# Order of the products of a near down block: pairs of output tiles, high halves first

## The chip, the cores and the metric

The kernel runs on one core of one Trainium2 chip. The metric is the device time of one execution in microseconds; three runs of the kernel before gave 1520.74, 1520.86 and 1521.19 us, the median being 1520.86 us. One more execution was recorded by the hardware profiler; all rows below are from that one.

## The reference, cut to what matters

The reference is a stack of layers over 256 tokens and 1024 features, all in float32. Six of its sublayers are feed-forwards of the same form, with 2816 inner features:

```python
def swiglu(h, w13, w2):
    gate, up = jnp.split(h @ w13, 2, axis=-1)
    return (jax.nn.silu(gate) * up) @ w2
```

Between them stand mixers: four kinds of token mixing in parallel, a gated linear recurrence, and an attention. The change touches the last product of the feed-forwards alone, `hidden @ w2`.

## The kernel before

Activations are held transposed: 128 features on the partitions, 256 tokens along the row. The float32 products are made from halves. A weight block `w` is split into a high half `w_hi` (the value rounded, made by ScalarE, line 666) and a low half `w_lo` (what is left, made by GpSimd, line 571, or by VectorE, line 1105). An activation tile is split in the same way, and both its halves lie side by side, 2 x 256 = 512 columns. A product of one 128x128 weight tile with one activation tile is then two matmuls (`three_products`, lines 1866 and 1867): the high half of the weight against both halves of the activation, 512 columns, and the low half of the weight against the high half of the activation, 256 columns. Both add into the same bank of PSUM, the second into its first 256 columns; VectorE adds the two halves of the bank when it takes the sum out. Below, H is a matmul of the first kind and L one of the second, each with its own weight load.

Weights stream through a ring of six slots (`RING`), one block of up to 128x1024 in each, loaded by SyncE's queue in the order in which TensorE uses them. A slot's semaphore `lo_ready` tells that both halves are made, `used` that TensorE is through with it.

A feed-forward (`ffn` of the TensorE program) goes over 22 chunks of 128 inner features. For a chunk c, `gate_up(c)` makes two tiles from the normed input `xn`: 16 pairs H L, eight for the gate and eight for the up projection, each tile in one bank of PSUM (banks 4 to 7, by turns). ScalarE and VectorE turn these into the hidden tile `hid[:, c]`, split into halves. `down(c)` then calls `near_products`, which multiplies the hidden tile by four of the eight output tiles: the near block, four weight tiles wide, adds into banks 0 to 3, one bank for each output tile d. The other four output tiles are made at the end of the feed-forward from far blocks (`far_products`), from the hidden tiles that are still in memory. The order of the steady part is written out in the code: for k from 0 to 18, `down(k)`, then `gate_up(k + 3)`. After that come `down(19)`, `down(20)`, the first far block, `down(21)`, and the other eleven far blocks. In all there are 6 x 22 = 132 near blocks, with four H and four L in each.

In `near_products` TensorE waits once for the block's low half (and, in `down`, once for the hidden tile), then issues the eight matmuls, and the last of them increments `used`. The order before is H0 L0 H1 L1 H2 L2 H3 L3, the number being the output tile.

Of the kernel before, what the change touches and what calls it, by code (L numbers as in the profile page):

```python
# [11 lines left out]
P = 128  # L12
SEQ = 256
# [5 lines left out]
NFC = FF // P  # L19
# [27 lines left out]
NEAR = HALF // P  # L47
# [21 lines left out]
def near_block(c):  # L69

    return NEAR_LAST if c == NFC - 1 else stored_down(c)
# [141 lines left out]
def slot(n):  # L213

    return n % RING
# [20 lines left out]
def nth_split(n):  # L236

    return SPLITS_SO_FAR[n]
# [34 lines left out]
def build(nc, x_in, blocks, consts, out):  # L273
    ctx = ExitStack()
    with ctx:
        def sb(name, shape, dt=F32):
            return ctx.enter_context(nc.sbuf_tensor(name, shape, dt))
# [6 lines left out]
        w_hi = sb("w_hi", [P, RING, BLK], F32R)  # L284
        w_lo = sb("w_lo", [P, RING, BLK], F32R)
# [19 lines left out]
        hid = nc.alloc_sbuf_tensor_at("hid", [P, NFC, 2, SEQ], F32R, offset=arena_at)  # L305
        ps = ctx.enter_context(nc.psum_tensor("ps", [P, 8, 512], F32))
# [1551 lines left out]
        def _(pe):  # L1858
# [5 lines left out]
            def three_products(where, hi, lo, both, opens, closes):  # L1864

                nc.tensor.matmul(where, hi, both.rearrange("p a t -> p (a t)"), start=opens, stop=False)  # L1866
                return nc.tensor.matmul(where[:, 0:SEQ], lo, both[:, 0, :], start=False, stop=closes)  # L1867
# [65 lines left out]
            def near_products(n0, c):  # L1933

                n = n0 + near_block(c)
                pe.wait_ge(lo_ready[slot(n)], nth_split(n))
                for d in range(NEAR):
                    wh, wl = (w[:, slot(n), d * P:d * P + P] for w in (w_hi, w_lo))
                    ins = three_products(ps[:, d, :], wh, wl, hid[:, c, :, :], c == 0, c == NFC - 1)
                ins.then_inc(used[slot(n)], 1)  # L1940

            def far_products(n0, i):
# [58 lines left out]
            def ffn(f, phase, total=total_squares):  # L2001
# [11 lines left out]
                def down(c):  # L2013
                    pe.wait_ge(h_ready, NFC * f + c + 1)
                    near_products(n0, c)
# [671 lines left out]
```

## Time and profile before

| | us |
|---|---|
| median of 3 runs | 1520.86 (1520.74 to 1521.19) |
| the profiled execution | 1521.21 |
| its span, first to last instruction | 1519.4 |
| TensorE matmuls busy | 1510.9 (99%) |
| TensorE weight loads busy | 1315.8 (87%) |
| VectorE busy | 1052.7 (69%) |
| GpSimd busy | 923.4 (61%) |
| ScalarE busy | 776.9 (51%) |
| TensorE clock granted | 1.000 of full speed over the span |

A matmul's recorded time runs from its start to its modelled end, and matmuls overlap in the pipeline, so the busy share of TensorE says only that there is nearly always one under way. What one matmul costs the engine is the distance from its start to the start of the next one; it is read from a timeline, in which starts are given to 0.01 us.

### The profile page before, as it was taken

The page shows a single profiled execution, that of the slowest core. Times are in us where ns is not written, and L with a number is a line of the kernel's source. Part 1 is how long each engine was busy: PE and PEld are TensorE (multiplying, and loading weights), DVE is VectorE, ACT ScalarE, POOL GpSimd, SP SyncE. Part 2 cuts the span into 40 slices and gives each one's busy share as a digit, 9 for nine tenths or more (in the row PEclk, how much of TensorE's full clock was granted, in tenths as well). Part 3 has the DMA queues.
Part 4 walks back from the last instruction along what each step waited for, and adds up shares of the span by engine and source line. Part 5 has one row for each costly group of instructions (what it writes and reads, how often), then busy time and mean ns, then how long its engine had stood idle before and what let it go on. Part 6 is the DMA issues. An engine that isn't in the chain of part 4 may idle for free.

```text
span 1519.4 us, 24540 instructions
## 1 busy us (share of the span) xinstructions
PE 1510.9 (99%) x9480; PEld 1315.8 (87%) x9480; DVE 1052.7 (69%) x1472; ACT 776.9 (51%) x1125; POOL 923.4 (61%) x1092
## 2 busy tenths in 40 slices
PE   9999999999999999999999999999999999999998
PEld 7888888888888888888899888888888887888887
DVE  7966555666986668976587986655466666797664
ACT  6554441123655455455567655456555456665542
POOL 4966520201687677876766687578776673168663
PEclk9999999999999999999999999999999999999999
DMA  8665633222565564665634565565555562346553
GB/s 302 209 196 183 205 99 115 85 79 86 199 212 183 168 215 160 192 205 165 228 126 167 186 210 185 183 215 187 162 189 189 186 207 94 138 156 207 188 165 119
DMA packets 113491, 263.64 MB, mean 174 GB/s; under 512 B 9184, under 2 KB 51296, under 8 KB 113248
## 3 DMA queue, kind: packets, MB, share of 16 engines
q1 hardware_dynamic: 113376, 262.09, 52.5%
q8 instruction: 75, 1.23, 0.3%
q14 instruction: 40, 0.33, 0.1%
HBM read 261.00 MB, written 1.05 MB: 172 GB/s over the span
## 4 chain that ended last, share of the span: by engine, by line
PE 74%; DVE 1%; ACT 0%; issue 0%; DVEq 0%; ACTq 0%
PE ps L1866 40%; PE ps L1867 21%; PE ps L1961 2%; PE ps L1982 2%; PE ps L1898 1%; PE ps L1899 1%; PE ps L1897 1%; PE ps L2434 1%; PE ps L2436 1%; PE ps L2435 1%; PE ps L2387 1%; PE ps L1997 0%; PE ps L1998 0%; PE ps L1996 0%; DVE arena L1812 0%; PE ps L1929 0%
## 5 line engine op out<-in xcount | busy, mean ns | idle before, releaser
L571 POOL TENSOR_TENSOR w_lo<-raw,w_hi 128x256 fp32r<-128x256 f32 x1056 | 902.4, 887 | 475.1 <-ACT w_hi L666 471.6
L1866 PE MATMUL ps<-xn,w_hi 128*128 128x512 f32 x2112 | 741.2, 393 | 0.4 <-POOL w_lo L571 0.2
L1867 PE MATMUL ps<-xn,w_lo 128*128 128x256 f32 x2112 | 591.4, 280 | 0.0
L666 ACT ACTIVATE w_hi<-raw 128x1024 fp32r<-128x1024 f32 (+1 forms) x516 | 475.5, 932 | 186.0 <-PE ps L1867 146.1
L1866 PEld LDWEIGHTS ps<-xn,w_hi 128*128 128x128 f32 x2112 | 395.1, 187 | 90.1 <-issue 0.7
L1867 PEld LDWEIGHTS ps<-xn,w_lo 128*128 128x128 f32 x2112 | 398.9, 189 | 0.2
L1866 PE MATMUL ps<-hid,w_hi 128*128 128x512 f32 x1056 | 379.4, 396 | 0.0
L1105 DVE TENSOR_TENSOR w_lo<-raw,w_hi 128x512 fp32r<-128x512 f32 (+1 forms) x245 | 284.8, 1163 | 32.5 <-ACT w_hi L666 27.6
L1867 PE MATMUL ps<-hid,w_lo 128*128 128x256 f32 x1056 | 297.1, 281 | 0.0
L1866 PEld LDWEIGHTS ps<-hid,w_hi 128*128 128x128 f32 x1056 | 198.4, 188 | 49.4
L1211 DVE TENSOR_TENSOR arena<-ps,low_part 128x512 f32<-128x512 f32 x132 | 90.8, 688 | 202.9 <-ACT low_part L783 202.9
L1867 PEld LDWEIGHTS ps<-hid,w_lo 128*128 128x128 f32 x1056 | 198.5, 188 | 0.0
L783 ACT ACTIVATE low_part<-ps 128x512 f32<-128x512 f32 x132 | 78.3, 593 | 163.8 <-PE ps L1867 163.6
L788 ACT ACTIVATE arena<-arena 128x256 f32<-128x256 f32 x132 | 55.3, 419 | 149.4 <-DVE arena L1221 149.4
L1221 DVE TENSOR_TENSOR arena<-arena,rstd 128x512 f32<-128x512 f32 x132 | 113.7, 861 | 4.5
L1913 PE MATMUL ps<-xs,raw 128*128 128x256 f32 x432 | 98.2, 382 | 0.0
L1231 DVE TENSOR_TENSOR h<-arena 128x256 f32<-128x256 f32 x132 | 91.5, 694 | 0.0
L1913 PEld LDWEIGHTS ps<-xs,raw 128*128 128x128 f32 x432 | 80.6, 190 | 12.2 <-issue 1.1
L1232 DVE TENSOR_TENSOR hid<-h,hid 128x256 fp32r<-128x256 f32 x132 | 86.0, 651 | 4.5
L1230 DVE TENSOR_TENSOR hid<-arena 128x256 fp32r<-128x256 f32 x132 | 60.7, 460 | 29.1 <-ACT arena L788 29.1
L1253 DVE SCALAR_TENSOR_TENSOR x<-ps,x 128x512 f32<-128x512 f32 x23 | 15.8, 686 | 59.6 <-PE ps L1867 59.6
L612 POOL TENSOR_TENSOR arena<-arena 128x512 f32<-128x512 f32 x4 | 4.5, 1113 | 77.5 <-DVE arena L1327 77.2
(345 smaller groups left out, 1305.8 us busy)
## 6 DMA issues: line engine op xcount, KB each, us to landing
raw<-blocks SPq DMA_DIRECT2D x418, 512.0 KB, 3.7
raw<-blocks SPq DMA_DIRECT2D x146, 256.0 KB, 3.5
cst<-consts SPq DMA_DIRECT2D x1, 2358.0 KB, 14.5
x<-x_in SPq DMA_DIRECT2D x4, 256.0 KB, 5.9
out<-x SPq DMA_DIRECT2D x4, 256.0 KB, 3.3
cst<-consts SPq DMA_DIRECT2D x1, 109.0 KB, 2.1
```

Of the source, the lines that this page charges most:

```text
L571: ins = nc.gpsimd.tensor_tensor(w_lo[:, slot(n), piece], raw[:, slot(n), piece], w_hi[:, slot(n), piece], ALU.subtract)
L666: nc.scalar.activation(w_hi[:, slot(n), cols], raw[:, slot(n), cols], ACT.Copy)\
L783: nc.scalar.activation(low_part[:, :, :], ps[:, b:b + 2, SEQ:], ACT.Copy).then_inc(low_taken, 1)
L1105: nc.vector.tensor_tensor(w_lo[:, slot(n), cols], raw[:, slot(n), cols], w_hi[:, slot(n), cols], ALU.subtract).then_inc(lo_ready[slot(n)], 1)
L1211: nc.vector.tensor_tensor(gate_up[:, :, :], ps[:, b:b + 2, 0:SEQ], low_part[:, :, :], ALU.add)\
L1221: nc.vector.tensor_tensor(gate_up[:, :, :], gate_up[:, :, :], over(rstd[:, :], 2), ALU.mult)\
L1230: nc.vector.tensor_tensor(hid[:, c, 0, :], gate_up[:, 1, :], gs, ALU.mult)
L1231: chain(nc.vector.tensor_tensor(h[:, :], gate_up[:, 1, :], gs, ALU.mult))
L1232: nc.vector.tensor_tensor(hid[:, c, 1, :], h[:, :], hid[:, c, 0, :], ALU.subtract)\
L1866: nc.tensor.matmul(where, hi, both.rearrange("p a t -> p (a t)"), start=opens, stop=False)
L1867: return nc.tensor.matmul(where[:, 0:SEQ], lo, both[:, 0, :], start=False, stop=closes)
L1913: ins = nc.tensor.matmul(where, raw[:, slot(n), k * P:k * P + P], xs[:, k, :], start=k == 0, stop=k == KD - 1)
```

## The change

In `near_products` the four output tiles are taken in two pairs. In a pair the two H come first, one after the other, then the two L: H0 H1 L0 L1 H2 H3 L2 L3. The waits, the increment on the last matmul, the operands, and the flags that open and close a bank's sum are the same. Nothing else is changed; far blocks and the gate and up blocks keep `three_products`.

```diff
                 pe.wait_ge(lo_ready[slot(n)], nth_split(n))
-                for d in range(NEAR):
-                    wh, wl = (w[:, slot(n), d * P:d * P + P] for w in (w_hi, w_lo))
-                    ins = three_products(ps[:, d, :], wh, wl, hid[:, c, :, :], c == 0, c == NFC - 1)
+
+                def high(d):
+                    return nc.tensor.matmul(ps[:, d, :], w_hi[:, slot(n), d * P:d * P + P],
+                                            hid[:, c, :, :].rearrange("p a t -> p (a t)"), start=c == 0, stop=False)
+
+                def low(d):
+                    return nc.tensor.matmul(ps[:, d, 0:SEQ], w_lo[:, slot(n), d * P:d * P + P], hid[:, c, 0, :],
+                                            start=False, stop=c == NFC - 1)
+
+                for d in range(0, NEAR, 2):
+                    for part in (high, low):
+                        for e in (d, d + 1):
+                            ins = part(e)
                 ins.then_inc(used[slot(n)], 1)
```

## Rows read from the trace of the kernel before

**Rows 1.** The page: span, and busy time of each engine.
```profile
span 1519.4 us, 24540 instructions
...
PE 1510.9 (99%) x9480; PEld 1315.8 (87%) x9480; DVE 1052.7 (69%) x1472; ACT 776.9 (51%) x1125; POOL 923.4 (61%) x1092
```
**Rows 2.** The page: the chain that ended last, by line.
```profile
PE ps L1866 40%; PE ps L1867 21%; PE ps L1961 2%; PE ps L1982 2%; PE ps L1898 1%; PE ps L1899 1%; PE ps L1897 1%; PE ps L2434 1%; PE ps L2436 1%; PE ps L2435 1%; PE ps L2387 1%; PE ps L1997 0%; PE ps L1998 0%; PE ps L1996 0%; DVE arena L1812 0%; PE ps L1929 0%
```
**Rows 3.** Instructions on the hidden tile: duration ns min/median/max, first and last start.
```profile
L1866 PE MATMUL ps<-hid,w_hi x1056: 389/394/423, 27.5 to 1515.1; 128*128 128x512 f32 x176
L1867 PEld LDWEIGHTS ps<-hid,w_lo x1056: 187/188/193, 27.5 to 1515.1; 128*128 128x128 f32 x176
L1867 PE MATMUL ps<-hid,w_lo x1056: 278/279/297, 27.7 to 1515.3; 128*128 128x256 f32 x176
```
**Rows 4.** One iteration by engine: length, busy us (instructions), PEclk, DMA share, GB/s.
```profile
90.34:97.33 6.99, 6.99 (x43) 6.13 (x42) 4.38 (x7) 3.55 (x5) 3.15 (x5) 1.00 0.77 248
```
**Rows 5.** Timeline of TensorE, a near block after a gate and up block: start, duration.
```profile
83.35 0.40 PE L1866 MATMUL ps<-hid,w_hi 128*128 128x512 f32 x1
...
83.71 0.39 PE L1866 MATMUL ps<-hid,w_hi 128*128 128x512 f32 x1
83.93 0.28 PE L1867 MATMUL ps<-hid,w_lo 128*128 128x256 f32 x1
84.05 0.42 PE L1866 MATMUL ps<-hid,w_hi 128*128 128x512 f32 x1
84.31 0.30 PE L1867 MATMUL ps<-hid,w_lo 128*128 128x256 f32 x1
84.44 0.39 PE L1866 MATMUL ps<-hid,w_hi 128*128 128x512 f32 x1
...
84.79 0.39 PE L1866 MATMUL ps<-xn,w_hi 128*128 128x512 f32 x1
```
**Rows 6.** Timeline of TensorE: the next near block's start, after 16 pairs.
```profile
90.34 0.40 PE L1866 MATMUL ps<-hid,w_hi 128*128 128x512 f32 x1
```
**Rows 7.** Timeline: first and last stalled near block, their starts and those after.
```profile
34.45 0.40 PE L1866 MATMUL ps<-hid,w_hi 128*128 128x512 f32 x1
...
35.88 0.39 PE L1866 MATMUL ps<-xn,w_hi 128*128 128x512 f32 x1
...
1480.40 0.40 PE L1866 MATMUL ps<-hid,w_hi 128*128 128x512 f32 x1
...
1481.83 0.40 PE L1866 MATMUL ps<-hid,w_hi 128*128 128x512 f32 x1
```
**Rows 8.** Timeline: two near blocks without a stall, and what starts after them.
```profile
161.64 0.40 PE L1866 MATMUL ps<-hid,w_hi 128*128 128x512 f32 x1
...
162.35 0.39 PE L1866 MATMUL ps<-hid,w_hi 128*128 128x512 f32 x1
...
162.70 0.39 PE L1866 MATMUL ps<-hid,w_hi 128*128 128x512 f32 x1
...
163.05 0.39 PE L1866 MATMUL ps<-hid,w_hi 128*128 128x512 f32 x1
...
585.45 0.40 PE L1866 MATMUL ps<-hid,w_hi 128*128 128x512 f32 x1
...
586.85 0.40 PE L1866 MATMUL ps<-xn,w_hi 128*128 128x512 f32 x1
```
**Rows 9.** Timeline: a run of 256-column matmuls, other weights each.
```profile
829.83 1.12 PE L1982 MATMUL ps<-xn,w_lo 128*128 128x256 f32 x8
830.78 2.08 PE L1982 MATMUL ps<-xn,w_hi 128*128 128x256 f32 x16
832.71 0.76 PE L1982 MATMUL ps<-xn,w_lo 128*128 128x256 f32 x5
```
**Rows 10.** Timeline: a run of 512-column matmuls, start of the first and thirteenth.
```profile
1064.21 0.39 PE L1996 MATMUL ps<-w_hi,kv_in 128*128 128x512 f32 x1
...
1066.93 0.39 PE L1996 MATMUL ps<-w_hi,kv_in 128*128 128x512 f32 x1
```

## The prediction, made before the changed kernel was run

> **What bounds the kernel now.** I read the page first, for which engine leaves no room. TensorE has a matmul under way in 1510.9 of 1519.4 us, and no other engine is busy for more than 69% of the span [rows 1]. The chain of waits says the same: its two largest entries are the lines of `three_products`, 40% and 21% [rows 2]. So the kernel is as long as the sum of the distances between TensorE's matmul starts, and a busy time doesn't show those, since matmuls overlap. I therefore went from the page to the timeline of TensorE in the steady part of a feed-forward and took start-to-start distances. One iteration (a near block and the gate and up block behind it) takes 6.99 us [rows 4, 6]: 83.35 to 84.79 for the eight matmuls of the near block, 1.44 us, and 84.79 to 90.34 for the 32 of gate and up, 5.55 us [rows 5, 6]. That is 0.347 us for a pair H L in gate and up (5.55 / 16), but 0.36 in the near block (1.44 / 4), with the same shapes.
>
> Then I looked for where the near block loses this. In the block at 83.35 the pair of output tile 0 takes 0.36 us (83.35 to 83.71), that of tile 1 0.34, that of tile 2 0.39 (84.05 to 84.44) and that of tile 3 0.35 [rows 5]. Tile 2 holds a stall: its H goes on to its L after 0.26 us where the H of tile 1 does so after 0.22, and its L to the next H after 0.13 against 0.12. The profile marks these two also as the longest of their kind: 0.42 and 0.30 us, the maxima over all matmuls on the hidden tile being 423 and 297 ns against medians of 394 and 279 [rows 3, 5]. The engine waits for no semaphore there, and weights and hidden tile are ready before the block starts.
>
> The stall is regular. Of the 132 near blocks 117 have it at this same place and take 1.43 to 1.44 us; the first and the last of them are the blocks at 34.45 and 1480.40 (1.43 us each) [rows 7]. The other 15 are without it and take 1.40 to 1.41 us: twelve are the blocks of chunks 20 and 21, whose neighbours are near and far blocks (that at 161.64 takes 1.41, its tile 2 only 0.35), and three are first blocks of a feed-forward, as that at 585.45 (1.40) [rows 8]. The same four output tiles and the same operands thus pass with the stall or without it, by what TensorE did just before. It is a matter of how matmuls and weight loads follow one another, not of a bank or an address alone.
>
> **The change part by part.** Work: each near block has eight weight loads and eight matmuls before and after, with the same operands. Nothing is added or removed, and no wait, increment or DMA moves. 132 x 4 x 2 = 1056 matmuls change their neighbours. All that can change is the sum of the distances in these blocks, now 117 x 1.435 + 15 x 1.405 = 189.0 us, 12% of the span.
>
> The new order has four kinds of steps in each half block: H to H, H to L, L to L, L to H. The trace of before has no such order, so I bound it.
> - The floor: in a run of 512-column matmuls, each with a weight load of its own, twelve distances take 1064.21 to 1066.93, 0.227 us each [rows 10]; in a run of 256-column ones 24 take 829.83 to 832.71, 0.120 us each [rows 9]. Four of each are 4 x 0.227 + 4 x 0.120 = 1.388 us, and gate and up with its alternation has the same, 4 x 0.347 = 1.388. If the new block came to this, it would save 117 x (1.435 - 1.388) + 15 x (1.405 - 1.388) = 5.5 + 0.3 = 5.8 us.
> - No gain: all 132 blocks as now, 0.
> - The other side: the stall is 0.39 - 0.35 = 0.04 us [rows 5, 8]. If each half had one, 117 x 0.04 + 15 x 0.08 = 5.9 us more.
> My value is a block without stall that still pays for being entered: 1.40 us, the lower of the two blocks of rows 8, between these and the floor and nearest to them. The reason to take the stall as gone is that H to H and L to L stand in the trace at their best distances, without a stall in any of the runs above, and that half the steps of the new block are of these kinds. The saving is 117 x (1.435 - 1.40) + 15 x (1.405 - 1.40) = 4.1 + 0.1 = 4.2 us.
>
> What could take it back: 0.035 us less in an iteration of 6.99 us means that weights must come 0.5% sooner. In the iteration of rows 4 VectorE is busy for 4.38, ScalarE for 3.55 and GpSimd for 3.15 us, and DMA is at 0.77 of its time; each has a fifth of the iteration or more to give, so I cost this at nothing. Were that cover gone, TensorE would wait for the splits and the saving would shrink to zero, not below. `used` rises on the last matmul of the block as before, so the loads behind it move with TensorE. The end of the kernel hangs on far blocks, which are not changed.
>
> The sum goes against the profiled execution: its span is 1519.4 us and its time 1521.21, 1.8 us around the span, which stay. 1521.21 is 0.35 above the median of 1520.86; off the median the forecast is 1520.86 - 4.2 = 1516.7 us.
>
> A rule of the Trainium skill speaks against any effect. A weight load of the hidden tile is recorded with 188 ns while a run of 256-column matmuls advances by 0.120 us [rows 3, 9], so loads here run beside matmuls that use the whole array. TensorE: Matmul & The Clock Gate, Part 3 (The mechanism), says that a load overlaps with matmuls in flight only when their row groups differ. By that rule none would overlap here, each matmul would pay for its own load in any order, and the time would be 1520.9; the trace disagrees with it, so it adds nothing to the chance of no change.
>
> **The rivals.**
> - *The stall belongs to entering the block and stays.* For it: it comes only after certain work in front of the block, gate and up above all, and that is not changed [rows 5, 8]. It would then hit whatever runs some 0.7 us into the block, in the new order the turn from L to H in the middle (2 x 0.227 + 2 x 0.120 = 0.69 us). Against it: it doesn't stand at the entry, but four matmuls behind it, and the blocks without it have the same waits. Time: 1520.9, give or take 1.5.
> - *The stall is paid twice (slower).* In the stalled block H of tile 1 moves on after 0.22 us, faster than any other H of the block, and the stall follows at the next H [rows 5]. If TensorE can run so only on something made ahead (weights or instructions) and pays for it afterwards, then the new order, which puts two H at this distance into each half, would pay in each half: 117 x 0.04 + 15 x 0.08 = 5.9 us, 1526.8 us. Against it: the runs at 0.227 and 0.120 us go on for twelve and 24 matmuls and pay nothing [rows 9, 10]. It decides when the block comes to over 1.46 us.
> - *Two L in a row don't cover a load (slower, and larger).* A load is recorded with 188 ns, an L moves on after 0.120 [rows 3, 9]. If H were needed to hide what is left, L to L would take up to 0.188 us: twice 0.068 in 132 blocks, 18 us, 1538.8 us. Against it: in the run of 256-column matmuls every one has a new weight tile and still takes 0.120 us [rows 9].
> - *All of it goes.* The block comes down to the floor of 1.388 us: 1515.1 us. For it: gate and up blocks reach it with the same alternation. Against it: no near block has, not even those without the stall [rows 8]. It is the lower end of the forecast's own case.
>
> **How the numbers follow.** A difference under 0.2% (3.0 us) can't be told from none by a measurement of this kernel; it takes a block of 1.41 us or less to pass it. Forecast (stall gone, 1515.1 to 1518.5 us): 0.52, of which 0.45 is faster by over 0.2% and 0.07 within. Stall stays or only moves: 0.29, of which 0.26 is the same, 0.01 faster and 0.02 slower. Stall in both halves or at other steps: 0.16, of which 0.13 is slower and 0.03 the same, since it can come in part. Uncovered loads: 0.03, all slower. Sums: faster 0.46, same 0.36, slower 0.18. The range goes from 1514.7, just under the floor, to 1524.0, which takes in the second case and half of the third; what lies outside is the full price of the stall in both halves, the uncovered loads and a gain over the floor, 0.15 together. The likeliest case's own range is 1515.1 to 1518.5 us.
>
> **What would show it.** In the timeline of TensorE after the change, eight matmuls on the hidden tile between gate and up blocks should take 1.39 to 1.41 us, the iteration 6.95 to 6.96 instead of 6.99, and the distances be near 0.227 (H to H) and 0.120 (L to L). The maxima of rows 3, 423 and 297 ns, should be gone or be left to few blocks. Gate and up blocks should keep 5.55 us; if they change, the block's exit acts on them, which I have at nothing. The prediction is wrong if the block keeps 1.43 us or more: at an unchanged 1.43 the stall belongs to the entry, with two long H's it is paid per half, and with L to L near 0.19 the loads are uncovered.

## The result, and the profile after

The changed kernel is slower: 1525.55 us (median of 8 runs, 1525.11 to 1526.07) against 1520.91 us (8 runs of the kernel before), a ratio of 1.0031 with a 95% interval of 1.0022 to 1.0039. That is 4.6 us more, where 4.2 us less was forecast. The profiled execution has a span of 1523.4 us, 4.0 more than the one before [rows 1]; it took 1525.19 us, a little under its median, and the one before, at 1521.21, a little over its own.

The page after, span and busy times: TensorE's busy time has grown by as much as the span, and that of no other engine has grown.
```profile
span 1523.4 us, 24540 instructions
...
PE 1514.9 (99%) x9480; PEld 1315.1 (86%) x9480; DVE 1048.4 (69%) x1472; ACT 776.9 (51%) x1125; POOL 920.8 (60%) x1092
```
The instructions on the hidden tile after, those of the near blocks (L1939 is H, L1943 is L; duration ns min/median/max): the H still has the maximum of rows 3, 423 ns; the L has lost its own, 286 instead of 297.
```profile
L1939 PE MATMUL ps<-hid,w_hi x528: 392/397/423, 27.1 to 1491.0; 128*128 128x512 f32 x176
...
L1943 PE MATMUL ps<-hid,w_lo x528: 276/279/286, 27.5 to 1491.3; 128*128 128x256 f32 x176
```
The timeline of TensorE after, over two iterations of the first feed-forward (start us, duration us; two H or two L in a row merge into one line, x2). It answers to rows 5 and 6.
```profile
62.14 0.63 PE L1939 MATMUL ps<-hid,w_hi 128*128 128x512 f32 x2
62.61 0.40 PE L1943 MATMUL ps<-hid,w_lo 128*128 128x256 f32 x2
62.84 0.63 PE L1939 MATMUL ps<-hid,w_hi 128*128 128x512 f32 x2
63.31 0.40 PE L1943 MATMUL ps<-hid,w_lo 128*128 128x256 f32 x2
63.55 0.39 PE L1866 MATMUL ps<-xn,w_hi 128*128 128x512 f32 x1
...
63.90 0.40 PE L1866 MATMUL ps<-xn,w_hi 128*128 128x512 f32 x1
...
64.25 0.40 PE L1866 MATMUL ps<-xn,w_hi 128*128 128x512 f32 x1
...
64.61 0.40 PE L1866 MATMUL ps<-xn,w_hi 128*128 128x512 f32 x1
...
64.96 0.40 PE L1866 MATMUL ps<-xn,w_hi 128*128 128x512 f32 x1
...
68.49 0.40 PE L1866 MATMUL ps<-xn,w_hi 128*128 128x512 f32 x1
...
68.85 0.40 PE L1866 MATMUL ps<-xn,w_hi 128*128 128x512 f32 x1
...
69.20 0.63 PE L1939 MATMUL ps<-hid,w_hi 128*128 128x512 f32 x2
69.67 0.40 PE L1943 MATMUL ps<-hid,w_lo 128*128 128x256 f32 x2
69.91 0.67 PE L1939 MATMUL ps<-hid,w_hi 128*128 128x512 f32 x2
70.41 0.40 PE L1943 MATMUL ps<-hid,w_lo 128*128 128x256 f32 x2
70.65 0.39 PE L1866 MATMUL ps<-xn,w_hi 128*128 128x512 f32 x1
...
71.69 0.39 PE L1866 MATMUL ps<-xn,w_hi 128*128 128x512 f32 x1
...
76.19 0.40 PE L1939 MATMUL ps<-hid,w_hi 128*128 128x512 f32 x1
```
Two things alternate. The near block at 62.14 is free of the stall and takes 1.41 us (to 63.55), as forecast. But the gate and up block behind it, whose code is unchanged, takes 5.65 us (63.55 to 69.20), where each took 5.55 before [rows 5, 6]: three of its pairs need 1.06 us (63.90 to 64.96), 0.353 each on average. They are not equal: from the starts at 63.90, 64.25, 64.61 and 64.96 they take 0.35, 0.36 and 0.35, and in this cycle of three the block goes on to its end, where each pair of a fast block behind its first two takes 0.346 to 0.347. The next near block has a stall, in its third H as before: the two H at 69.91 reach the next L only after 0.50 us (70.41), where the two at 69.20 need 0.47. It takes 1.45 us, and the gate and up block behind it is fast again: 5.54 us, three pairs in 1.04 (70.65 to 71.69). Below, *fast* pace means 0.347 us for a pair H L, and *slow* pace the cycle of three with its mean of 0.353.

Together two iterations take 14.05 us (62.14 to 76.19) instead of 2 x 6.99 = 13.98, and there are 57 such twos in the 114 iterations: 57 x 0.07 = 4.0 us. Summed over the starts of all 114 iterations in the two traces, the gate and up blocks take 5.4 us more and the near blocks 0.9 less, 4.5 together, and the rest of the span is 0.5 us shorter. 56 of the 114 gate and up blocks take 5.65 us; before, none did. The first and the last of them lie between these starts, and a third in the fourth feed-forward:
```profile
35.45 0.39 PE L1866 MATMUL ps<-xn,w_hi 128*128 128x512 f32 x1
...
41.09 0.40 PE L1939 MATMUL ps<-hid,w_hi 128*128 128x512 f32 x1
...
860.71 0.39 PE L1866 MATMUL ps<-xn,w_hi 128*128 128x512 f32 x1
...
866.36 0.40 PE L1939 MATMUL ps<-hid,w_hi 128*128 128x512 f32 x1
...
1478.74 0.39 PE L1866 MATMUL ps<-xn,w_hi 128*128 128x512 f32 x1
...
1484.38 0.40 PE L1939 MATMUL ps<-hid,w_hi 128*128 128x512 f32 x1
```
5.64 to 5.65 us each. The one at 860.71 follows the near block of chunk 0, the one at 35.45 that of chunk 1. The split of an up block goes by turns to GpSimd and VectorE, by even and odd chunks; the slow blocks are even ones in some feed-forwards and odd ones in others, so it isn't that turn which makes them slow. Nor is it the slot of the ring: an iteration takes three of the six, so slots go by turns too, but the slow gate blocks of the sixth feed-forward and fast ones of the second lie in the same slot 0.

The work of the other engines beside a block doesn't make it slow either. All 56 slow blocks take 5.648 or 5.649 us, while over the same blocks the DMA share goes from 0.06 to 0.78, and GpSimd is busy for 0.06 to 1.00 of the time. Two of them (length, then busy us and instructions of TensorE, its weight loads, VectorE, ScalarE and GpSimd, then the clock, the DMA share and GB/s):
```profile
147.87:153.52 5.65, 5.65 (x34) 4.91 (x33) 3.80 (x7) 1.91 (x4) 0.36 (x1) 1.00 0.72 230
987.19:992.84 5.65, 5.65 (x35) 4.90 (x33) 4.06 (x6) 2.33 (x4) 5.12 (x6) 1.00 0.06 21
```

### The profile page after: what moved, and what is told of

Its sections match the earlier page's. It is cut to its first block, busy times and chain, and to the rows that moved or that the text cites. A ratio compares the mean times of both kernels' runs of the same rounds, so it can differ in the third digit from the quotient of the medians.

```text
span 1523.4 us, 24540 instructions
## 1 busy us (share of the span) xinstructions
PE 1514.9 (99%) x9480; PEld 1315.1 (86%) x9480; DVE 1048.4 (69%) x1472; ACT 776.9 (51%) x1125; POOL 920.8 (60%) x1092
## 4 chain that ended last, share of the span: by engine, by line
PE 74%; DVE 1%; ACT 0%; issue 0%; DVEq 0%; ACTq 0%
PE ps L1866 33%; PE ps L1867 17%; PE ps L1939 7%; PE ps L1943 3%; PE ps L1971 2%; PE ps L1992 2%; PE ps L1899 1%; PE ps L1897 1%; PE ps L1898 1%; PE ps L2444 1%; PE ps L2446 1%; PE ps L2445 1%; PE ps L2397 1%; PE ps L2008 0%; PE ps L2006 0%; PE ps L2007 0%
## 5 line engine op out<-in xcount | busy, mean ns | idle before, releaser
L1866 PE MATMUL ps<-hid,w_hi 128*128 128x512 f32 x528 | 185.4, 393 | 0.0
L1939 PE MATMUL ps<-hid,w_hi 128*128 128x512 f32 x528 | 168.2, 400 | 0.0
L1867 PE MATMUL ps<-hid,w_lo 128*128 128x256 f32 x528 | 147.3, 279 | 0.0
L1943 PEld LDWEIGHTS ps<-hid,w_lo 128*128 128x128 f32 x528 | 99.2, 188 | 26.0
L1866 PEld LDWEIGHTS ps<-hid,w_hi 128*128 128x128 f32 x528 | 98.9, 187 | 23.2
L1943 PE MATMUL ps<-hid,w_lo 128*128 128x256 f32 x528 | 105.5, 280 | 0.0
```

Of the source, the lines that this page charges most:

```text
L1939: return nc.tensor.matmul(ps[:, d, :], w_hi[:, slot(n), d * P:d * P + P], hid[:, c, :, :].rearrange("p a t -> p (a t)"), start=c == 0, sto ...
L1943: return nc.tensor.matmul(ps[:, d, 0:SEQ], w_lo[:, slot(n), d * P:d * P + P], hid[:, c, 0, :], start=False, stop=c == NFC - 1)
```

## The experiments

Each times a kernel against the one before on the same chip, in two or three rounds; one profiled execution of each was read as above. All but e8, which computes one product too many and lets it be overwritten, issue the same matmuls in another order, or with a wait or a tile elsewhere. The base is named with each; the orders are written with H and L as in the code above.

**e1, e2: half of the change.** Base: before. In `near_products`:
```diff
-H0 L0 H1 L1 H2 L2 H3 L3
+H0 L0 H1 L1 H2 H3 L2 L3      (e1_second_half)
+H0 H1 L0 L1 H2 L2 H3 L3      (e2_first_half)
```


> Only the second pair of output tiles in the new order: H0 L0 H1 L1 H2 H3 L2 L3. Theory A (rhythm): the near block leaves TensorE in one of several rhythms, by the sizes of its last matmuls, and the gate and up block behind it keeps the rhythm in which it is entered, 5.55 us or 5.65. The block leaves as the new order does, so about half of the gate and up blocks take 5.65 us: 1524 to 1527 us. Theory B (neighbours: the other engines' accesses, shifted by some 10 ns, collide with the gate and up block): any shift will do, so some blocks at 5.65 too. Theory C (addresses of the weights read side by side): no forecast for the time; stalls move with the output tiles.

> Only the first pair of output tiles in the new order: H0 H1 L0 L1 H2 L2 H3 L3. Theory A: the block is left as before, by H L H L, so all gate and up blocks take 5.55 us, and the near block at most 1.44: 1517 to 1521 us. Theory B: the block's length changes as well, so some gate and up blocks take 5.65 us and the time is over 1522.


Measured: e1 1520.93 us (ratio 1.0001, 0.9991 to 1.0010), e2 1525.45 us (1.0031, 1.0019 to 1.0043). This is the reverse of what theory A forecast: the new order in the last half does nothing to the time, and in the first half alone it costs all that the change costs. The timeline of e1 shows a near block with the stall, in the second half now in the new order:
```profile
62.19 0.40 PE L1939 MATMUL ps<-hid,w_hi 128*128 128x512 f32 x1
...
62.89 0.67 PE L1939 MATMUL ps<-hid,w_hi 128*128 128x512 f32 x2
63.39 0.40 PE L1943 MATMUL ps<-hid,w_lo 128*128 128x256 f32 x2
63.63 0.39 PE L1866 MATMUL ps<-xn,w_hi 128*128 128x512 f32 x1
```
1.44 us from 62.19 to 63.63, with 0.50 from the third H to the L behind the fourth, as in the block at 69.91 above; the gate and up blocks of e1 are all fast. In e2 near blocks of 1.41 and 1.44 us and gate and up blocks of 5.65 and 5.55 alternate, as in the changed kernel. What remains of theory A is that a pace is carried on from block to block; what sets it is the beginning of the near block.

**e3: all H first.** Base: before.
```diff
-H0 L0 H1 L1 H2 L2 H3 L3
+H0 H1 H2 H3 L0 L1 L2 L3
```


> All four H, then all four L: H0 H1 H2 H3 L0 L1 L2 L3. Theory A: the block is left by four L; the rhythm behind it is the same in every iteration or alternates, 5.55 or 5.65 us, so the time is near one of 1516 (all 5.55, near block 1.40), 1521 to 1526 (mixed) or 1530 (all 5.65). Theory B: as mixed, by chance of the shift. The stall of the near block, if tied to the change from L to H inside the block, is gone: 1.39 to 1.41 us.


Measured: 1528.93 us (1.0054, 1.0038 to 1.0071). No near block of the steady part has the stall (1.42 us), and 111 of the 114 gate and up blocks are slow, 5.64 to 5.65 us. So the slow pace doesn't need the alternation, and a near block without stall isn't worth anything by itself: the slow pace costs 0.09 to 0.10 us an iteration, three times the stall.

**e4: the tiles of a pair swapped.** Base: the changed kernel.
```diff
-H0 H1 L0 L1 H2 H3 L2 L3
+H1 H0 L1 L0 H3 H2 L3 L2
```


> The sizes in the new order, but the output tiles of each pair swapped: H1 H0 L1 L0 H3 H2 L3 L2. Theory A: sizes alone count, so the near blocks alternate between 1.41 and 1.45 us and the gate and up blocks between 5.65 and 5.55 as in the changed kernel: 1525 to 1526.3 us. Theory C (addresses): another pattern, and a time more than 1 us away from the changed kernel's.


Measured: 1525.36 us (1.0031, 1.0019 to 1.0042), with the same alternation. The sequence of sizes counts, not which tile it is.

**e5: the two orders by turns.** Base: before; chunks of odd number in the new order.
```diff
-                for d in range(NEAR):
...
+                pairs = ((0, 1), (2, 3)) if c % 2 else ((0,), (1,), (2,), (3,))
+                for pair in pairs:
+                    for part in (high, low):
+                        for e in pair:
...
```


> Even chunks in the order before, odd ones in the new order. Theory R (rhythm): TensorE has a fast rhythm (0.347 us for a pair H L) and a slow one (0.353). A first half block in the new order, entered fast, has no stall and leaves the gate and up block behind it slow (5.65 us); a block entered slow, in either order, leaves it fast. So odd near blocks take 1.41 us with 5.65 behind, even ones are entered slow and take 1.40 to 1.41 with 5.55 behind: two iterations 14.02 us against 13.97 before, 57 x 0.043 = 2.4 us more, 1523.2 us. Rival B (neighbours shifted in time): even blocks keep the stall (1.44 us), since they are as before.


Measured: 1523.61 us (1.0017, 1.0008 to 1.0027). The timeline of e5, an even block and the odd one behind it:
```profile
55.72 0.40 PE L1939 MATMUL ps<-hid,w_hi 128*128 128x512 f32 x1
...
57.13 0.39 PE L1866 MATMUL ps<-xn,w_hi 128*128 128x512 f32 x1
...
62.68 0.63 PE L1939 MATMUL ps<-hid,w_hi 128*128 128x512 f32 x2
...
64.09 0.39 PE L1866 MATMUL ps<-xn,w_hi 128*128 128x512 f32 x1
...
69.74 0.40 PE L1939 MATMUL ps<-hid,w_hi 128*128 128x512 f32 x1
```
The even block, in the order before, takes 1.41 us without the stall that it has in 117 of 132 cases before [rows 7], because the block ahead left TensorE slow; behind it gate and up are fast (57.13 to 62.68, 5.55). The odd block takes 1.41 and leaves 5.65 behind it (64.09 to 69.74). Two iterations come to 14.02 us, as theory R had it. Rival B has fallen: the even blocks are as before and lost the stall. Whether an order stalls, and what it leaves, hangs on how it is entered.

**e6: a wait moved.** Base: the changed kernel.
```diff
                 for k in range(FFN_STEPS):
+                    pe.wait_ge(halves_added, NFC * f + k + LEAD - 1)
                     down(k)
```
with the same wait taken out of `gate_up` for these chunks.


> New order, and the wait for halves_added, which stood at the first weight load of each gate block, is moved ahead of the near block in front. Rival W (waits): the stall and the rhythm come from TensorE's sequencer, which meets two waits at the gate block while the fifth matmul of the near block runs; with one wait there the stalls go or move and the gate and up blocks take 5.55 us: 1520.5 us or less. Theory R without waits: the same two kinds of blocks as in the changed kernel, 1525.5 us within 0.7.


Measured: 1525.48 us (1.0030, 1.0018 to 1.0042), the same alternation. This wait is not the cause; the other one at the gate block, for the low half of its weights, stayed where it was, and the trace doesn't show when TensorE's sequencer meets a wait.

**e7: one pair swapped in the gate block.** Base: the changed kernel.
```diff
-gate: H0 L0 H1 L1 H2 L2 ... H7 L7
+gate: H0 L0 L1 H1 H2 L2 ... H7 L7
```


> New order in the near blocks, and in each gate block of the steady part the second of the eight pairs is issued L before H, so that two L and two H follow each other there. Theory R: what counts is the sequence of sizes in TensorE, wherever it stands, so this turn can change the rhythm of the matmuls behind it; the share of slow gate and up blocks changes and the time is over 1 us away from 1525.5 (1520.5 if all are fast, 1531 if all are slow). Rival B: rhythm comes from outside TensorE, 1525.5 us within 1 and the same alternation.


Measured: 1528.11 us (1.0047, 1.0032 to 1.0062). The alternation is gone: 108 of the 114 near blocks take 1.42 us, and every gate and up block 5.63 to 5.64, for one turn inside the gate block, where nothing but TensorE's own sequence changed. Rival B, which had the same alternation, has fallen here too.

The run shows one thing more. All these near blocks but the first of each feed-forward are entered at the slow pace, in the same order and from the same kind of pairs as the stalled ones of the changed kernel, and yet only three of them stall. A near block of the common kind in e7, and one of the three:
```profile
61.94 0.40 PE L1866 MATMUL ps<-xn,w_hi 128*128 128x512 f32 x1
...
62.30 0.40 PE L1866 MATMUL ps<-xn,w_hi 128*128 128x512 f32 x1
...
62.65 0.40 PE L1866 MATMUL ps<-xn,w_hi 128*128 128x512 f32 x1
...
62.99 0.63 PE L1944 MATMUL ps<-hid,w_hi 128*128 128x512 f32 x2
...
64.41 0.39 PE L1866 MATMUL ps<-xn,w_hi 128*128 128x512 f32 x1
...
406.89 0.40 PE L1866 MATMUL ps<-xn,w_hi 128*128 128x512 f32 x1
...
407.26 0.40 PE L1866 MATMUL ps<-xn,w_hi 128*128 128x512 f32 x1
...
407.61 0.63 PE L1944 MATMUL ps<-hid,w_hi 128*128 128x512 f32 x2
...
409.05 0.39 PE L1866 MATMUL ps<-xn,w_hi 128*128 128x512 f32 x1
```
The first comes two pairs after the long one of the cycle (0.36 from 61.94 to 62.30) and takes 1.42 us; the second comes one pair after it (0.37 from 406.89 to 407.26) and takes 1.44, as the stalled block of the changed kernel at 69.20 comes one pair after the 0.36 from 68.49 to 68.85. So it is not the pace alone that decides about the stall, but the place in its cycle at which the near block begins.

**e8: one more L ahead of the gate block.** Base: the changed kernel.
```diff
+                    if c >= LEAD:
...
+                        nc.tensor.matmul(ps[:, bank_of(c), 0:SEQ], w_lo[:, slot(n), 0:P], xn[:, 0, 0, :], start=True, stop=True)
                     feature_tiles([(n0 + gate_block(c), bank_of(c))])
```


> New order, and one more L (its result is overwritten by the gate product that opens the bank) between each near block and the gate block behind it. Its price is 114 x 0.12 = 13.7 us. Theory R: an entry by three L is another entry, so the alternation goes: all gate and up blocks fast is 1520.9 + 13.7 - 1 to 2 = 1533 to 1534 us, all slow 1544 to 1546. Rival B: the alternation stays, 1525.5 + 13.7 = 1539 us.


Measured: 1537.60 us (1.0111, 1.0096 to 1.0126), between the fast forecast of theory R and that of rival B. The extra L costs its 0.12 us. Slow and fast gate and up blocks still alternate, as rival B had it and against theory R; but the stall is gone from the near blocks (1.41 and 1.42 us), 57 x 0.03 = 1.7 us that rival B's sum kept. That doesn't bring rival B back, which e5 and e7 refute. As in e7, the near blocks entered slow come two pairs after the long one. The run shows that the stall is not needed for the return to the fast pace: here TensorE returns to it without one, as it does in e5.

**e9, e10: the up block's end.** Base: before, with the near blocks as before.
```diff
-up: ... H6 L6 H7 L7
+up: ... H6 H7 L6 L7          (e9_up_ends_hhll)
+up: ... H6 L6 L7 H7          (e10_up_ends_lh)
```


> Near blocks in the order before; in the up blocks the last two of the eight pairs are issued H H L L. Theory R (two rhythms, carried over from block to block; a near block entered fast in the order before pays the stall of 0.03 us and goes on fast): the near block is entered in another state, as in the run by turns, where it took 1.41 us without stall and left the gate and up block fast; if so, 114 x 0.025 = 3 us less, 1518 us. If the turn only makes the end of the up block slow, the time is 1520 to 1522. Rival S (the stall belongs to the fifth matmul of a near block in the order before, whatever comes ahead of it): 1521 us.

> Near blocks in the order before; in the up blocks the last of the eight pairs is issued L before H, so the near block is entered from an H. Theory R: the near block is entered in another state, as above: 1518 us if the stall goes and the rhythm stays fast, 1525 to 1531 if the gate and up blocks turn slow in half or in all iterations. Rival S: 1521 us.


Measured: e9 1519.26 us (0.9990, 0.9980 to 0.9999), e10 1518.60 us (0.9984, 0.9975 to 0.9994). A near block of e9 and the start of the gate block behind it:
```profile
62.16 0.40 PE L1866 MATMUL ps<-hid,w_hi 128*128 128x512 f32 x1
...
63.56 0.40 PE L1866 MATMUL ps<-xn,w_hi 128*128 128x512 f32 x1
```
Untouched near blocks lose their stall (1.40 us in e9, 1.41 in e10) because the work ahead of them ends in another way, and leave the gate and up blocks at the fast pace but for the turn itself (5.57 and 5.56 us). Rival S has fallen.

**e11: the turn in the middle.** Base: before.
```diff
-H0 L0 H1 L1 H2 L2 H3 L3
+H0 L0 H1 H2 L1 L2 H3 L3
```


> Near blocks in the order H0 L0 H1 H2 L1 L2 H3 L3. Theory R: the stall comes with the third H after H L H L and puts TensorE back into the fast rhythm; here the third H comes one place earlier. With the stall: gate and up blocks fast, 1520 to 1522 us; without it: near blocks of 1.41 us and gate and up blocks slow in half or all iterations, 1524 to 1531 us. A saving needs both, no stall and a fast exit, which no order had so far when entered fast: 1518 us, one chance in six.


Measured: 1517.82 us (0.9980, 0.9971 to 0.9989): 3.1 us less than before, and faster than both kernels: the case that was given one chance in six. The timeline of e11:
```profile
62.52 0.40 PE L1939 MATMUL ps<-hid,w_hi 128*128 128x512 f32 x1
62.75 0.28 PE L1943 MATMUL ps<-hid,w_lo 128*128 128x256 f32 x1
62.87 0.62 PE L1939 MATMUL ps<-hid,w_hi 128*128 128x512 f32 x2
63.33 0.40 PE L1943 MATMUL ps<-hid,w_lo 128*128 128x256 f32 x2
63.57 0.39 PE L1939 MATMUL ps<-hid,w_hi 128*128 128x512 f32 x1
...
63.92 0.40 PE L1866 MATMUL ps<-xn,w_hi 128*128 128x512 f32 x1
...
69.48 0.40 PE L1939 MATMUL ps<-hid,w_hi 128*128 128x512 f32 x1
```
The near block takes 1.40 us and the gate and up block 5.56: no stall and a fast pace behind, which the changed kernel has together only at four first blocks of a feed-forward. The iteration is 6.96 us against 6.99 [rows 4], and 114 x 0.03 = 3.4 us is the gain within the rounding. It is less than the stall: at the trace's full resolution the near block takes 1.404 instead of 1.437 us, but the gate and up block behind it 5.557 instead of 5.549, so 0.025 us an iteration is left.

**e12: H H L L everywhere.** Base: the changed kernel, its steady gate and up blocks in the same order.
```diff
-gate, up: H0 L0 H1 L1 ...
+gate, up: H0 H1 L0 L1 H2 H3 L2 L3 ...
```


> New order in the near blocks, and the steady gate and up blocks in the same order, two pairs each: H H L L over two weight tiles of one bank. Theory R1: H H L L runs in the slow rhythm by itself (a near block of 1.413 us without stall is 4 x 0.353), so the 114 gate and up blocks take 5.65 us and the near blocks 1.41: 1520.9 + 114 x (0.10 - 0.024) = 1529.6 us. Theory R2: it has a rhythm of its own at the floor of 0.347 a pair, 5.55 us, near blocks 1.39 to 1.41: 1517 to 1518 us.


Measured: 1522.59 us (1.0010, 1.0001 to 1.0020). Neither theory is right: H H L L settles into a third pace. Near blocks take 1.42 us, gate and up 5.58, between the fast 5.55 and the slow 5.65.

**e13: the hidden tiles moved.** Bases: the changed kernel, and the one before.
```diff
+        sb("shift", [P, 192])
         ARENA = 17100
```


> New order, with the hidden tiles (and all of the arena) 768 bytes further on in each partition. Rival C (addresses: the stall and the slow rhythm come from weights and activations read side by side from places that collide): the alternation changes, and the time moves by over 1 us from 1525.5. Theory R (only the sequence of sizes counts): the same alternation of near blocks of 1.41 and 1.45 us, 1525.5 us within 0.7.

> The order before, with the same shift of 768 bytes. Rival C: the stall at the third output tile goes or moves to another one, and the time leaves 1520.9 by over 1 us. Theory R: the stall stays where it is, near blocks of 1.44 us, 1520.9 us within 0.7.


Measured: 1525.57 us (1.0031, 1.0020 to 1.0042) and 1521.04 us (1.0002, 0.9992 to 1.0013), and in both traces the same kinds of blocks as unmoved; only first blocks of a feed-forward differ here and there. For this shift, rival C is out.

## Why the prediction was wrong

Its steps one by one:
- *TensorE sets the end, and start-to-start distances are what to sum.* Right: the kernel's time moved with the near, gate and up blocks in every run.
- *Nothing but the distances in the 132 near blocks can change.* This is the step that failed. The prediction says "All that can change is the sum of the distances in these blocks", and at its end: "Gate and up blocks should keep 5.55 us; if they change, the block's exit acts on them, which I have at nothing." 56 of them went to 5.65 us: 56 x 0.10 = 5.6 us that the sum didn't have. The near blocks saved, by the two iterations above, (1.41 + 1.45) / 2 = 1.43 against 1.435, under 1 us in all. The term was put at nothing without a reason: that no work, wait or operand of these blocks changes leaves out the order of the matmuls ahead of them. The trace of before held a small sign: the three gate and up blocks behind unstalled first blocks take 5.556 to 5.557 us, the other 111 take 5.549 or 5.550.
- *The stall goes.* Right in every second near block, entered fast. Wrong in the other half: entered from a slow block, one pair after the long one of its cycle, the new order has the stall (1.45 us), and its price is the one that was read from rows 5 and 8, 0.03 to 0.04 us.
- *The chosen value, 1.40 us, by the nearest row.* The unstalled blocks came to 1.41 with the new order, and e11 reached 1.40 by another. The size was good; what it took for granted, that a block without stall costs nothing behind it, was not: even in e11, where the pace stays fast, 0.008 of the 0.033 us come back in the gate and up block.
- *The rivals.* The slower one that was priced (the stall in both halves, 1526.8 us) came near the measured time by accident: no near block shows two stalls, and its decisive sign, blocks of over 1.46 us, is missing. Uncovered loads are out too: two L in a row advance by about 0.12 us in the block at 62.14 (0.23 from 62.61 to 62.84). That "the same operands thus pass with the stall or without it, by what TensorE did just before" was read rightly from the trace, and it holds the answer: what carries a past into the near block can carry it out of it as well. Only the entrance was thought through.
- *The bounds.* The range ended at 1524.0 us and had only prices of steps inside the near block, 0.04 us for a stall. The price stood behind it, 0.10 us a block, some 6 ns on average in each of 16 pairs that no line of the change touches.

What the experiments establish: the slower time is the slow pace of gate and up blocks behind near blocks that begin H H and were entered fast (e2 alone has all of it, e1 none); the sequence of matmul sizes on TensorE sets it (e4, e7, e9 to e11), and not the wait that was moved (e6), the order of the tiles (e4) or, for the one shift that was tried, the place of the hidden tiles (e13). Contention with the other engines doesn't fit e5 and e7, nor the equal lengths of the 56 slow blocks beside very unequal work; a run of TensorE without the other engines wasn't made. What stays open: what inside TensorE holds the pace, and why a start with H H brings on the slow one. Two states don't describe it: the place in the slow cycle counts (e7), in e3 near blocks entered slow leave slow again, the first near block of a feed-forward, in the changed kernel too, may pass without stall and leave a fast pace, and e12 has a third pace.

## What to carry to other kernels

Where an engine is busy all the time, look at the distance from start to start not only in the edited block but also in the unchanged blocks behind it, over several iterations: a change of order can pay off where it is made and cost more in what follows. A stall that comes or not by what went before tells that the sequence has a memory; then no local sum decides, and the cheap way is to try a few orders, here the turn in the first half, in the middle or at the end (1525.5, 1517.8 and 1520.9 us). Before giving a saving from a removed stall, ask what state the stall left behind.

## What the hardware showed beyond what was expected

With the clock granted at 1.000 in both traces (the level of 2.4 GHz), the same row of 32 matmuls in a gate and up block ran in two ways: behind its first two pairs either at 0.346 to 0.347 us for each pair of 512 and 256 columns, or in a cycle of 0.350, 0.361 and 0.349 us with a mean of 0.353, and kept to it up to the end. In the order H H L L (e12) two such pairs took 2 x 0.349 (5.58 / 16). A single swap of two neighbours in the second pair of the gate block (e7) set the slow pace for the rest of the block. The Trainium skill, TensorE: Matmul & The Clock Gate, Part 2 (Back-to-back issue gap), gives a warm gap of columns / 2.4 + 2.5 ns for the isolated matmul and says that in a stream with weight loads it over-counts long matmuls; an estimate from this formula is 0.216 + 0.109 = 0.325 us for such a pair. The trace doesn't agree that the formula over-counts: with a weight load for each matmul even the fast pace is 0.022 us above the estimate.
